# An encoder layer's PEER heads among the query slabs, and small transfers on GpSimd's queue

## What is computed

```python
x1 = _layer_norm(DN_ALPHA * x + mix, ln1_g, ln1_b)
# _peer(x1, peer_wq, peer_keys, peer_u, peer_v):
q = (x1 @ wq).reshape(T, 8, 2, 128)
s = einsum('thcd,hcnd->thcn', q, keys)
v1, i1 = top_k(s[:, :, 0], 16); v2, i2 = top_k(s[:, :, 1], 16)
top_s, pos = top_k(all 256 sums v1 + v2, 16)      # per head
idx = the 16 experts i1 * 128 + i2 of each head   # 128 per token
g = softmax(top_s)
a = einsum('td,tkd->tk', x, u_tab[idx])
y = einsum('tk,tkd->td', gelu(a) * g, v_tab[idx])
```

## Time and profile before

| | us |
|---|---|
| median of 3 runs | 3700.64 |
| lowest, highest | 3700.53, 3703.7 |
| profiled execution | 3716.53 |
| its span, first to last instruction | 3714.6 |
| mean granted clock of TensorE | 0.822 |
| busy PE, DVE, POOL, ACT | 2464.5, 2764.5, 1237.7, 332.5 |
| moved by DMA | 1332.41 MB, 359 GB/s over the span |

### The profile page before, as it was taken

The page is one execution under the profiler, slowest core; times in us unless marked ns, Lnnn a source line. Parts: engine busy times, 40 slices in busy tenths (PEclk is TensorE's granted clock), DMA queues, the critical chain, the costliest instruction groups (busy, mean ns, idle before and its releaser), DMA issues.

```text
span 3714.6 us, 30313 instructions
## 1 busy us (share of the span) xinstructions
PE 2464.5 (66%) x11208; PEld 1898.9 (51%) x11208; DVE 2764.5 (74%) x3210; ACT 332.5 (9%) x832; POOL 1237.7 (33%) x1273
## 2 busy tenths in 40 slices
PE   7798799987965776969989999999978000000000
PEld 7687689544733454545577878777767000000000
DVE  5331220979989997787789889985557999999988
ACT  1212211000002221001010000000000000000000
POOL 2420000122123332222222223222222577777772
PEclk9899899998986667989999999999999555555555
DMA  8774355898999999989999999999999999999998
GB/s 248 223 230 124 136 189 187 272 391 331 353 391 344 410 409 383 422 358 397 422 422 423 423 423 423 423 418 423 423 384 410 409 400 408 409 410 383 393 373 350
DMA packets 296882, 1332.41 MB, mean 359 GB/s; under 512 B 69728, under 2 KB 135808, under 8 KB 145312
## 3 DMA queue, kind: packets, MB, share of 16 engines
q0 software_dynamic: 138624, 945.22, 63.1%
q1 hardware_dynamic: 125376, 371.83, 27.1%
q10 hardware_dynamic: 32736, 13.44, 1.4%
HBM read 1282.60 MB, written 57.20 MB: 361 GB/s over the span
## 4 chain that ended last, share of the span: by engine, by line
PE 34%; DMA 25%; DVE 19%; POOL 9%; issue 9%; ACT 1%; SPq 1%; ACTq 1%; DVEq 0%; POOLq 0%
PE low L1561 18%; DMA arena<-in_ut 16%; PE low L1902 10%; DVE arena L1377 6%; POOL arena L612 5%; POOL arena L621 5%; DVE acc L1393 4%; DMA arena<-in_peer_v,arena 3%; DMA arena<-in_w 2%; DMA arena<-in_peer_u,arena 2%; PE low L1635 1%; PE acc L1635 1%; DMA arena<-y_scratch_b 1%; DVE low L1393 1%; DVE arena L1195 1%
## 5 line engine op out<-in xcount | busy, mean ns | idle before, releaser
L1393 DVE SCALAR_TENSOR_TENSOR acc<-arena,acc 128x2048 f32<-128x2048 f32 x443 | 1042.9, 2354 | 266.1 <-DMA arena<-in_peer_v,arena 229.1
L1561 PE MATMUL low<-arena 128*128 128x192 f32 (+1 forms) x4096 | 1063.2, 419 | 102.1 <-DMA arena<-in_w 76.8
L1902 PE MATMUL low<-arena 128*128 128x256 f32 x4096 | 908.8, 383 | 103.3 <-DMA arena<-in_ut 103.2
L1561 PEld LDWEIGHTS low<-arena 128*128 128x128 f32 x4096 | 736.0, 195 | 378.4 <-DMA arena<-in_w 74.4
L1902 PEld LDWEIGHTS low<-arena 128*128 128x128 f32 x4096 | 781.3, 192 | 230.6 <-DMA arena<-in_ut 109.8
L612 POOL DMA_INDIRECT arena<-in_peer_v,arena x576 | 573.4, 995 | 909.2 <-DVE acc L1393 740.9
L1377 DVE SCALAR_TENSOR_TENSOR arena<-arena,acc 128x2048 f32<-128x2048 f32 x320 | 725.0, 2285 | 118.4 <-DMA arena<-in_peer_u,arena 110.9
L612 POOL DMA_INDIRECT arena<-in_peer_u,arena x320 | 320.0, 1000 | 1197.3 <-DVE arena L1377 862.4
L1393 DVE SCALAR_TENSOR_TENSOR low<-arena,low 128x2048 f32<-128x2048 f32 x126 | 296.6, 2354 | 29.6 <-issue 13.6
L621 POOL DMA_INDIRECT arena<-expert_scratch,arena x256 | 260.7, 1018 | 79.2 <-issue 79.2
L873 ACT COPY arena<-low 128x256 f32<-128x256 f32 x128 | 47.6, 372 | 957.5 <-DMA expert_scratch<-arena 635.3
(11 more groups left out here) (274 smaller groups left out, 1688.0 us busy)
## 6 DMA issues: line engine op xcount, KB each, us to landing
arena<-in_w SPq DMA_DIRECT2D x128, 1024.0 KB
arena<-in_ut SPq DMA_DIRECT2D x128, 1024.0 KB
expert_scratch<-arena SPq DMA_DIRECT2D x64, 256.0 KB
arena<-in_peer_v,arena POOLq DMA_INDIRECT x576
arena<-toeplitz_scratch SPq DMA_DIRECT2D x64, 128.0 KB, 4.1
arena<-c_scratch SPq DMA_DIRECT2D x64, 128.0 KB, 4.7
bias_scratch<-distance_scratch SPq DMA_DIRECT2D x1, 5120.0 KB, 23.2
x_scratch<-arena ACTq DMA_DIRECT2D x5, 1024.0 KB
```

What stands on the lines that cost most here:

```text
L1393: stt(held, slot[j], wv_, held, ALU.mult, ALU.add).then_inc(used, 1)
L1561: ins = mm(L[n % 2][:, 0:width], wring[n % 2][:, k, :], rhs(k), start=k == 0, stop=k == KT - 1)
L1902: ins = mm(L[j % 4][:, 0:NSD], ud[j % 4][:, k, :], lane(catB, k)[:, P:NB], start=k == 0, stop=k == KT - 1)
```

## The change

Five things are done.

1. Tile 0's heads are scored in quarters between the query slabs (`quarter`, on PE and ACT), and DVE takes each pair of heads with `decode_head` as soon as its quarter is copied. No rows stand between them. `SLOT_FROM` lets slots 2 and 3 in from row 2.
2. Tile 1's heads move ahead of the scan, with two rows before each, and 20 rows after them; 64 rows in one piece stand between the scan and the wait for y. So 36 rows stand ahead of the scan (before 42), 113 ahead of the wait for y (99), and 130 ahead of attention (116).
3. Tile 2's heads are scored in quarters among the N_WB slabs and decoded head by head: 11 rows, then four times 9 rows and two heads.
4. `u_move` and the stores of y (`y_store`) are issued by GpSimd, between gathers: `u_move` ahead of gathers 0, 3, 6 and 10, `y_store` ahead of gathers 68, 75, 82 and 89. The first part of u is stored ahead of the N_WA slabs.
5. Five loads for the early layer norms are spread over 24 blocks of the dense stage rather than issued at once, and ACT's part of the first norm stands 4 blocks earlier. `chosen(t, h)` is the count of `idx_ready` that belongs to a head.

The diff, cut to its core:

```diff
-SLOT_FROM = [0, 0, TOPK, TOPK, STEPS[0] + 6, R_U2 + 16]
+SLOT_FROM = [0, 0, 2, 2, STEPS[0] + 6, R_U2 + 16]
+U_ROWS = [3, 6, 10]
+Y_ROWS = [68, 75, 82, 89]
+def chosen(t, h=PH - 1):
+    return {0: h + 1, 1: PH + 1, 2: PH + 2 + h, 3: 2 * PH + 2, 4: 2 * PH + 3}[t]
...
# SP
-                if j == EB - 12:
-                    early_sums()
+                if j in range(EB - 36, EB - 11, 6):
+                    next(sums)
...
# GpSimd
+            def u_move(part):
+                pool.wait_ge(u_stored[1][part], 16)
+                pool.wait_ge(x1_ready, 2)
+                for k in range(SL):
+                    pool.dma_start(U8B[k * SG:(k + 1) * SG, 16 * part:16 * part + 16],
+                                   uscrB.rearrange("(g h) s c -> s h g c", h=SG)[SL - 1 - k][:, 16 * part:16 * part + 16]
+                                   ).then_inc(u_moved[1], 16)
+            def y_store(b):
+                pool.wait_ge(y_out[1], b + 1)
+                for t in range(SL):
+                    pool.dma_start(yscrB.rearrange("(g h) s c -> s h g c", h=SG)[t][:, 16 * b:16 * b + 16, :],
+                                   U8B[t * SG:(t + 1) * SG, 16 * b:16 * b + 16, :]).then_inc(y_stored[1], 16)
...
+            u_move(0)
             for i in range(R_V3 - EAHEAD):
+                if i in U_ROWS:
+                    u_move(U_ROWS.index(i) + 1)
+                if i in Y_ROWS:
+                    y_store(Y_ROWS.index(i))
                 gather(i)
...
# ACT
+            def quarter(t, c):
+                act.wait_ge(score_done, 4 * t + c + 1)
+                if t == NGA and not c:
+                    act.wait_ge(x1_stored, 16 * NT)
+                ins = nc.scalar.copy(scored[t][:, 512 * c:512 * c + 512], L[2 + c % 2])
+                ins.then_inc(quarter_out, 1)
...
             ln1_out(1)
+            u_store(1, uPB, uscrB, N_UB[1] + 1, 0, 2, 0)
             mixed_a(N_WA)
-            scores(0)
+            quarter(0, 3)
             scores(1)
...
-            products(106, EB - 2)
+            products(106, EB - 6)
             ln2(0, 0)
-            products(EB - 2, EB)
+            products(EB - 6, EB)
             ln2(1, 1)
...
# DVE
-            dve.wait_ge(score_out, 1)
             for h in range(PH):
+                if h % 2 == 0:
+                    dve.wait_ge(quarter_out, h // 2 + 1)
                 head(0, h)
                 decode_head(0, h)
-                if h:
-                    rows(2)
             logits(0)
             link.zero()
-            rows(28)
+            for h in range(PH):
+                rows(2)
+                head(1, h)
+            rows(20)
...
-            for h in range(PH):
-                rows(3)
-                head(1, h)
-            rows(20)
+            rows(64)
             dve.wait_ge(y_moved[1], 16)
...
-            rows(53)
+            rows(11)
             dve.wait_ge(keys_in, 48)
-            dve.wait_ge(score_out, 3)
             for h in range(PH):
-                rows(5)
+                if h % 2 == 0:
+                    rows(9)
+                    dve.wait_ge(quarter_out, 4 + h // 2 + 1)
                 head(2, h)
-            decode(2, rows)
+                decode_head(2, h)
...
# PE
+            def quarter(t, c, qp, base, keys):
+                first = (N_WA, N_WB)[t // 2]
+                c0 = MIXCOL[t] - base
+                pe.wait_ge(slab_out, first + 4 * c + 4)
+                pe.wait_ge(keys_in, 32 + 16 * (t // 2))
+                if c >= 2:
+                    pe.wait_ge(quarter_out, 4 * (t // 2) + c - 1)
+                for q in range(4):
+                    ins = mm(L[2 + c % 2][:, P * q:P * q + P], qp[:, 4 * c + q, c0:c0 + P],
+                             keys[:, P * (4 * c + q):P * (4 * c + q) + P], start=True, stop=True)
+                ins.then_inc(score_done, 1)
...
             for i in range(16):
-                slab(N_WA + i, ca, NA)
+                slab(N_WA + i, ca, NA, queries(i, 0, mixA, 0, keysA))
...
             for i in range(16):
-                slab(N_WB + i, cb, NB)
+                slab(N_WB + i, cb, NB, queries(i, 2, mixB, NA, keysB))
```

More of the change, by code:

```diff
@@ L634, in _ @@
                     sum_store(1)
-            pool.wait_ge(idx_ready, PH + NT - 1)
+            pool.wait_ge(idx_ready, chosen(NT - 1))
             for b in range(2):
@@ L882, in mixed_a @@
                 for i in range(16):
+                    if first == N_WA and i and i % 4 == 0:
+                        quarter(0, i // 4 - 1)
                     act.wait_ge(slab_done, first + i + 1)
@@ L1001, in _ @@
             ln1_out(4)
-            slabs_out(N_WB, 16, mixB, NB)
-            for t in range(NGA, NT):
+            for i in range(16):
+                if i and i % 4 == 0:
+                    quarter(2, i // 4 - 1)
+                out_of(N_WB + i, mixB[:, i, :], L[i % 2][:, 0:NB])
+            quarter(2, 3)
+            for t in range(NGU, NT):
                 scores(t)
@@ L1890, in _ @@
             for i in range(16):
-                slab(N_WB + i, cb, NB)
-            pe.wait_ge(slab_out, N_WB + 16)
-            pe.wait_ge(keys_in, 48)
-            for t in range(NGA, NT):
+                slab(N_WB + i, cb, NB, queries(i, 2, mixB, NA, keysB))
+            quarter(2, 3, mixB, NA, keysB)
+            for t in range(NGU, NT):
                 scores(t, mixB, NA, keysB, low)
```

51 lines of the change are left out of this document (28 added, 23 removed).

## The result

The changed kernel is slower. Its median is 3743.69 us against 3702.17 us of the kernel before, four runs each; the ratio is 1.0114, with a 95% interval of 1.0098 to 1.0129, or +42 us. The forecast was +10 us, 3711, with a range to 3734: the sign was right, the size was missed by a factor of four.

A forecast was written before the change was run, and what follows sets the result against it. Row transfers (DMA) bound the kernel from about 650 us, except three stretches where DVE does. Later attention +24, 14 rows more −35, tile 2's heads +18, the rest +3: +10 us, 3711, range 3676 to 3734.

The forecast's parts named there:

- Heads of tile 0, and the scan: Early heads among query slabs: first near 579, row 16 near 768; scan begins at 829, ends at 901.
- The way to y: Scan to attention: y's groups 31 us apart, row 113 at 1117, attention at 1188, 24 us later with 14 rows more.
- Heads of tile 2: Heads among N_WB slabs: DVE full while DMA lacks rows, 7 rows lost, +18 us, bounds 0 and +28.
- part 4: Tile 2's heads among N_WB: 27 rows where 43 fit, less 5 landed and some 4 for loads; +18 us.
- The rest: ACT's queue 0, spread loads 0, ACT's earlier norm and GpSimd's extra idx_ready waits +3 us, between 0 and +8.
- Faster, if y is not later: Rival: y's groups keep 25 us, attention at 1166, sum −12, 3689; chance 0.30.
- No change: Rival: y half-way late (+12), or rows lost beside N_WB made good; sum −2, 3699; chance 0.27.
- The heads beside N_WB starve DMA: Rival: heads hold DVE 20 us, slots fill in 16, 11 rows lost, attention +30; +26, 3727; chance 0.12.
- It does not do what it says: Rival: tile 0's heads held by matmuls or keys, row 16 moves to 780; counted among the slower cases.
- GpSimd's own price: Rival: GpSimd's 64 direct transfers each wait out a row instruction of 2.3 us; +37, 3748; chance 0.04.
- DMA's packets in turn: At y's transfers: DMA engines serve queues packet by packet, so small packets get less; alone, the sum equals the forecast's.
- part 1: Tile 0's heads among query slabs: six heads, 60 us of DVE, leave the stretch behind 667; row 16 stays at 768.

The follow-up runs named there:

- e2: Kernel before with only tile 2's heads moved among the N_WB slabs, by quarters, 11 rows then four times 9 rows and two heads; ratio 1.0085, +31 us.
- e1: Changed kernel with tile 2's heads back beside the dense stage, 53 rows ahead; ratio 1.0045 to the kernel before.
- e3: Changed kernel with 50 rows in place of 64 between the scan and the wait for y; ratio 1.0121 to the kernel before.
- e4: Changed kernel with u_move and the stores of y issued by ACT again; ratio 1.0069 to the kernel before.
- e6: e1 with 14 rows in place of one ahead of the second early norm, and u_move and y's stores on ACT's queue; ratio 0.9991 to the kernel before.
- e10: e6 with four heads of tile 1 ahead of the scan and four behind, 46 rows ahead of the scan; ratio 0.9992 to the kernel before.
- e12: e11 with u_move ahead of gathers 7, 14, 21, y's stores ahead of 76, 82, 88, 94, and 54 rows ahead of the scan; ratio 0.9995 to the kernel before.
- e9: e6 with tile 1's heads back behind the scan and 56 rows in a piece ahead of it; ratio 1.0100 to the kernel before.
- e11: e9 with u_move and y's stores on GpSimd's queue, the latter ahead of gathers 80, 86, 92 and 98; ratio 1.0024 to the kernel before.

## Why the forecast was wrong

**Heads of tile 0, and the scan.** Right. First head at 578.51 (forecast 579), row 16 at 767.8 (768), the scan at 827.63 (829), its end at 901.2 (901). The gathers stood behind u's stores as told.

**The way to y.** Nearly right: last copy of y at 1032.35 (1031), row 113 at 1124 (1117), attention 33 us later (24). The groups were not even, 30, 40 and 36 us apart where 31 had been told, but in sum they fit. Two small terms were missed: seven us up to row 113, and the stretch from y's first operation to attention, which took 73.1 us and not 70.4.

**Heads of tile 2.** Here the forecast failed. It counted 7 rows lost, +18 us, with an upper bound of 11. It was 13: 342 rows stood where 341 + 14 were due. At 2.5 us a row that is 33 us; e2 has the same 13 rows and +31 us for this part alone. The step that failed is the pair of credits in part 4. The count had 43 rows that fit and 27 that are worked, 16 short, and took off five rows landed in the slots and some four for the dense stage's first loads. The measured 13 leave three of these nine. The loads could not fill the hole, since SP issues them only when all scores are done: `in_ut` was issued at 1902, and PE waited 14.41 us for it, as the 14.33 before. The slots were no gain either, because gathers stand ahead of DVE in any case: 347 had been issued against 342 rows begun when the dense stage began, and 345 against 341 in the kernel before. DMA had nothing else to fetch for 118 us at a share of 0.76, 28 us of transfers lost. The 22 rows ahead were mis-sized as well. They were to end at about 1760, which gives them 2.1 us each; the heads began at 1784, so that the hole was shorter than the 143 us of the forecast.

**The rest.** Given +3 (0 to 8); it was +10. The dense stage took 1007 us for the 997 before. The place can be told: between 1882 and 2850 the changed kernel has at each moment as many gathers issued, within three, as the kernel before had 33.9 us earlier. At 2900 it has four fewer, 10 us of rows. These 50 us hold the two early norms and the wait of 7.91 us behind ACT's step, which the kernel before has not. No run takes this wait alone out of the changed kernel, so that it makes up most of the 10 us is argued. In e1, with more rows won, the wait is 29 us.

Per term the sum is now +33 − 35 + 33 + 10 = +41 us, with 42 measured. Its −35 and +33 are rows counted in the two profiles at 2.5 us each; no run measures the −35 alone. Of the 31 us by which the forecast's +10 was short, 15 lie in the heads of tile 2, 9 in the way to y and 7 in the rest.

**The rivals.** *Faster, if y is not later*: e3 had y at 1090.65 and attention at 1161, only by doing fewer rows, and was no faster. The rival's premise, both at once, was never reached: in the eleven kernels with 113 rows ahead of y it never came before 1118. *No change* needed y half-way or the rows beside N_WB made good; attention came 33 us later and 13 rows were lost. *The heads beside N_WB starve DMA* was the right mechanism and had 0.12, as an extreme of the forecast; it should have been its centre, and even its 11 rows were two too few. *It does not do what it says* is ruled out by the first head at 578.51 and row 16 at 767.8. *GpSimd's own price*: each of its transfers took 0.57 us, so that the warning of the Trainium skill ("SBUF — State Buffer", section "A bandwidth-pool intuition that's wrong (but worth ruling out)") of about 3100 ns is not what happens here. The queue did cost 6 to 17 us (e4, e6), by another way than the one priced. *DMA's packets in turn* (the Trainium skill, "DMA: Bandwidth & Descriptors", section "Queues, rings and completion order"): that small transfers suffer beside 8 KB rows is seen in ACT's issues of y's stores, 5.79 us for the first eight in the kernel before and 20 to 39 in e4; that it is due to the order of packets no run here shows.

What the argument lacked is an account of DMA over the whole stretch. It had a share of 0.95 from the first row to the end of attention; the 60 us of DVE work that part 1 takes out could bring at most the missing 5% of 818 us, 41 us. Of what is missing in the changed kernel 11 us lie in the scan and 8 at attention's start, where DVE is full of other work (shares of 0.85 and 0.89 in its table), and 14 in 655–760 (0.87), which holds the waits for u's stores and tile 1's heads.

No kernel of these experiments beat the kernel before; e6, e10 and e12 are even with it.

## What to carry to other kernels

Where transfers are the bound, ask of each moved piece of work what DMA does in the place that it leaves and in the place that it comes to. Work taken from a place where DMA was full brings nothing, and the same work put where DMA was full, in pieces longer than the buffers ahead can cover (here 20 us of heads against five slots of about 3 us), costs the overrun. Before crediting a hole with other transfers, look up what releases them.

A wait that is short today can eat a gain: the norm behind the last block held DVE 8 us, and 29 us once 12 rows had been won. Look for the next fixed point behind a gain.

## What the hardware showed

- Eight transfers of 192-byte pieces took ACT 4.5 to 10.5 us to issue in the kernel before, where heads stand between the rows, and 13 to 39 us in e4, e6, e9 and e10 at places where more rows ran beside them (one group of y in e9 took 11.6 and one 6.05). On GpSimd's queue, which also issues the rows, eight took 4.5 to 4.6 us in every run.
- A busy DMA alone does not hold up a single store. In e12 ACT's stores of u took 0.37 and 0.42 us to issue, with a DMA share of 1.02 in 684–699 and 1.04 in 700–714:

```profile
688.64 0.37 ACTq L718 DMA_DIRECT2D u_scratch_b<-arena  x1
...
710.00 0.42 ACTq L718 DMA_DIRECT2D u_scratch_b<-arena  x1
```

  The 14.59 us of e9 fall in the same place, at a share of 1.02, and are those of a store directly behind eight small transfers in its own queue. Such transfers in an engine's queue beside a busy DMA are what goes with the long issues; the mechanism is not shown. Keep them off an engine whose other work is waited for: taking them off ACT gave 28 us from e9 to e11. It is no rule without exception: in e4 and e6 ACT took 20 to 39 us over y's stores and DVE waited 25.47 and 23.79 us for y, and both kernels were faster than the same with GpSimd's queue.
- The last 128 rows, with the same code, ran at 324 to 326 us on one chip and at 338 to 344 us on three others. Comparing profiles that were not taken side by side needs marks that leave such a stretch out.
